# A third token tile whose low and high parts share one stationary operand

## The chip, the cores and the metric

The kernel runs on one core of a Trainium2 chip. The metric is the device time of one execution in microseconds (us), the median over runs. TensorE (PE) does the matmuls, with its weight loads (PEld) beside them; VectorE (DVE) and ScalarE (ACT) do the elementwise work; GpSimd (POOL) and SyncE (SP) mostly issue DMAs.

## What is computed

One inference step of a two-layer trunk for 256 prompt tokens and 8 x 8 sample tokens, 320 in all, model width 1024, in fp32. Each layer has a mixing sub-layer and a channel sub-layer, each followed by a LayerNorm of the scaled residual:

```python
mix, nb_a, nb_b, h_last = token_mixing(x, ...)      # convolution, recurrent and cross-attention branches,
                                                    # merged by gates, then merged @ w_mix_out
x = layer_norm(ALPHA * x + mix, ln1_g[l], ln1_b[l])
if l % 2 == 0:
    f = swiglu(x, w_ff_gate[j], w_ff_up[j], w_ff_down[j])   # hidden width 2816
else:
    f = moe_swiglu(x, w_router[j], ...)                     # top 2 of 8 experts
x = layer_norm(ALPHA * x + f, ln2_g[l], ln2_b[l])
```

## The kernel before

**Precision by parts.** An fp32 operand is cut into a high part (a cast to fp32r, made by ScalarE) and a low part (the operand less its high part, made by VectorE). A product is three matmuls that add up in PSUM: high x high, high x low, low x high. The product low x low is left out. The weights come in units of 128 rows x 1024 columns (512 KB) through a ring of 6 slots, which SyncE fills (L643). `make_hi` (L543) and `make_lo` (L551) split a unit into `wh` and `wl`, of which there are 3 (`SPLITS`): the high part of a unit may be made when the matmuls with the unit three before it are done.

**Two kinds of products.** Most products (`blocks`, L1660 to L1662) give their result with features on the partitions and the 320 tokens in the free dimension. Three of them have tokens on the partitions, so that the residual and the LayerNorm can work along a row; `rows_of` (L1665) does these: merged @ w_mix_out of each layer (8 units, called "mix") and hidden @ w_ff_down of layer 0 (22 units, "down"). In these the activations are the stationary operand and the weights the moving one.

**Token tiles.** `TOK = [0, 128, 192]` are the first tokens of three tiles of 128. Tile 2 holds tokens 192 to 319. Its first 64 rows (`DUP`) are tokens that tile 1 has too, and what is computed for them is used by nobody; the 64 sample tokens are its rows 64 to 127. For each unit, tile and half of 512 columns, `unit` issues three matmuls of 128x512 (L1673 high x high, L1674 high x low, L1675 low x high): 18 for a unit. Each tile and half has a PSUM bank, 6 in all. The tiles are taken in the order `TURN = (2, 0, 1)`. For all units but the last three (`LAST = 3`) the loop over tiles is the inner one; then each tile in turn takes its last three units and is closed, so that VectorE can begin with tile 2 while TensorE is at tiles 0 and 1.

**What follows a tile's close.** `residual` on VectorE (L1155) does, for each tile in the same order, x = ALPHA * x + bank for the two halves (L1161), the statistics (L1112, L1114), a wait for ScalarE's square root (`layer_norm_std`, L622; its square root L628, and a first tiny activation at L625 that brings the function table in early), the reciprocal (L1119), and the normalisation (L1120). TensorE then transposes x (`turn_x`, L1702), all 8 blocks of a tile behind each other, in the order of `TURN`; the later tiles overwrite the columns of the duplicated tokens. VectorE goes on with the splits of the next units (L555) and with `turned_lo`, which makes gain and bias (`xaff`, L1149) and the low part `xTl` (L1142) of the transposed rows.

**The stationary operands.** `mgh` and `mgl` (merged, [128, 8, 320]) and `hTh` and `hTl` (hidden, [128, 22, 320]) are separate tensors. ScalarE makes the high parts, one copy of 128x320 each (L976 for merged, L993 and L996 for hidden), VectorE the low parts in one subtraction each (`merged_lo` L1403, `hidden_lo` L1169). merged is made while TensorE is at the last branch product ("yb", 8 blocks of 24 matmuls), hidden during the feed-forward stretch of layer 0 (gate and up, 44 units of 24 matmuls). All these buffers lie in one arena by offsets written out by hand; tensors whose lives do not overlap share a place.

The order of the work is written out: `make_plan` counts the steps of TensorE, and `split_for(step)` on ScalarE and VectorE puts the splits of the coming units at fixed places in those engines' order.

Of the kernel before, what the change touches and what calls it, by code (L numbers as in the profile page):

```python
# [36 lines left out]
P = 128  # L37
# [35 lines left out]
MEAN_AFTER = 2  # L73
LAST = 3
# [194 lines left out]
def trunk(nc, x0, x0T, chan, rows, hist, stream, router_w, router_b, experts,  # L269
# [5 lines left out]
    with ExitStack() as ctx:  # L275
# [83 lines left out]
        v, mgh = share(JB * T, ("mgh", KT, T))  # L359
        ua, ig, ig_flat = blocks_of(v, JA, LEN_A), blocks_of(v, JB, T), v  # L360
# [16 lines left out]
        v, meml, mgl = share(JB * T, ("meml", KT, N_MEM), ("mgl", KT, T))  # L377
# [17 lines left out]
        hTh, hTl = cut_r("hTh", FT * T, FT), cut_r("hTl", FT * T, FT)  # L395
        dsig = cut(2 * T, 2)
        dlin = cut(2 * T, 2)
        dh = cut(2 * T, 2)
        xaff = cut(3 * T, 3)

# [63 lines left out]
        hgh_ready, hgl_ready = sem("hgh_ready"), sem("hgl_ready")  # L464
        mgh_ready, mgl_ready = sem("mgh_ready"), sem("mgl_ready")
# [156 lines left out]
        def layer_norm_std(act, n):  # L622

            act.wait_ge(eps_ready, 1)
            act.activation(turn_top[0:1], ones[0:1, 0:1], ACT.Sqrt)  # L625
# [197 lines left out]
        def _(act):  # L823
# [30 lines left out]

            for l in range(DEPTH):
# [117 lines left out]
                for n in range(KT):  # L973
                    split_for(tile_of(l, "yb", n).done)
                    act.wait_ge(mg_ready, KT * l + n + 1)
                    act.copy(mgh[:, n], mg[:, n]).then_inc(mgh_ready, 1)  # L976
                split_for(last_rows(l, "mix", KT))
                layer_norm_std(act, 2 * l)
                if l % 2 == 0:
# [4 lines left out]
                    for f in range(FT):  # L984
# [5 lines left out]
                        if f:  # L990
                            split_for(tile_of(l, "u", f - 1).done)
                            emptied(act, l, "u", f - 1)
                            act.copy(hTh[:, f - 1], dh[:, (f - 1) % 2]).then_inc(dhh_ready, 1)  # L993
                    split_for(tile_of(l, "u", FT - 1).done)
                    emptied(act, l, "u", FT - 1)
                    act.copy(hTh[:, FT - 1], dh[:, (FT - 1) % 2]).then_inc(dhh_ready, 1)  # L996
                    split_for(last_rows(l, "down", FT))
                    layer_norm_std(act, 2 * l + 1)
# [94 lines left out]
        def _(dve):  # L1093
# [61 lines left out]
            def residual(n, l, name):  # L1155

                for t in TURN:
                    for c in range(2):
                        m = 2 * t + c
                        filled(dve, l, name, m)  # L1160
                        frees(dve.scalar_tensor_tensor(out=x[:, t, 512 * c:512 * c + 512],  # L1161
                                                       in0=x[:, t, 512 * c:512 * c + 512], scalar=ALPHA,
                                                       in1=bank(l, name, m), op0=ALU.mult, op1=ALU.add), l, name, m)
                    for c in range(2):
                        emptied(dve, l, name, 2 * t + c)
                    spread(n, x, t)
                    scaled(n, x, t)

            def hidden_lo(f):  # L1169

                dve.wait_ge(dhh_ready, f + 1)
                dve.tensor_tensor(hTl[:, f], dh[:, f % 2], hTh[:, f].bitcast(F32), ALU.subtract)\
                   .then_inc(dhl_ready, 1)
# [933 lines left out]
```

## Time and profile before

| | us |
|---|---|
| median of 3 runs | 2064.41 (2064.2 to 2066.55) |
| the profiled execution | 2060.36 |
| its span, first to last instruction | 2058.6 |
| TensorE busy | 1923.8 (93%) |
| VectorE busy | 1488.0 (72%) |
| ScalarE busy | 1057.3 (51%) |
| mean granted TensorE clock | 0.973 of full speed |

How to read the rows further down: a line such as L1673 is one of the kernel. In a row of the busy time by stretch stand the stretch, its length, then for PE, PEld, DVE, ACT and POOL the busy us and the number of instructions in brackets, then the granted TensorE clock, the DMA engines' busy share and GB/s. A row of the timeline gives the start, the duration, and in square brackets the idle time before it with what ended it. Matmuls are pipelined: the duration of one is longer than the distance to the start of the next. A row of a group gives after the bar the busy time in us and the mean ns of one instruction. In the chain a row gives start, us on the chain, and what.

### The profile page before, as it was taken

Reading aid. Unit: us, or ns where it says so; the run is one execution under the profiler, and the core shown is the slowest. Engines: PE = TensorE matmul, PEld = TensorE weight load, DVE = VectorE, ACT = ScalarE, POOL = GpSimd, SP = SyncE. Lnnn points to the kernel's source line nnn. Section 1 sums busy time; section 2 is a strip of 40 time slices with the busy share of each in tenths; the row PEclk is TensorE's granted clock in tenths of the full one; section 3 lists DMA queues with packets and bytes.
Section 4 is the critical chain, followed back from the end, with each engine's and each line's share of the span. In section 5 each row is a group of like instructions: output and inputs, shape, how many; then the busy total and the mean of one; then the engine's idle time right before and its main releaser. Section 6 shows DMA issues by size and latency. Waiting matters only on the chain.

```text
span 2058.6 us, 27972 instructions
## 1 busy us (share of the span) xinstructions
PE 1923.8 (93%) x10429; PEld 1636.0 (79%) x10430; DVE 1488.0 (72%) x2049; ACT 1057.3 (51%) x1154; POOL 95.9 (5%) x156
## 2 busy tenths in 40 slices
PE   7999889899997999988979999999999999999990
PEld 7889789799986978988966677878788888876670
DVE  6987685665525888657567567888888888886664
ACT  4453643334322435364335446677777677765541
POOL 1100000000001000000000001010101010100000
PEclk9999999999999999999989999999999999999995
DMA  7643334354432553533437558898989898986413
GB/s 259 221 171 132 131 121 151 105 170 153 145 131 95 186 198 122 185 112 126 135 146 264 198 211 321 338 379 338 375 330 384 334 377 337 377 338 241 179 59 120
DMA packets 118741, 447.43 MB, mean 217 GB/s; under 512 B 10384, under 2 KB 10384, under 8 KB 118144
## 3 DMA queue, kind: packets, MB, share of 16 engines
q1 hardware_dynamic: 112416, 424.97, 56.5%
q0 software_dynamic: 6240, 21.33, 2.9%
q8 instruction: 53, 0.87, 0.2%
q14 instruction: 32, 0.26, 0.0%
HBM read 437.52 MB, written 11.36 MB: 218 GB/s over the span
## 4 chain that ended last, share of the span: by engine, by line
PE 76%; DVE 13%; issue 5%; ACT 5%; DMA 1%; SPq 0%; DVEq 0%; POOL 0%; ACTq 0%; POOLq 0%
PE psum L1896 11%; PE psum L1898 11%; PE psum L1897 10%; PE psum L1660 8%; PE psum L1661 8%; PE psum L1662 8%; PE psum L1646 4%; PE psum L1902 3%; PE psum L1903 3%; DVE wl L555 2%; DVE arena L1103 2%; PE psum L1673 2%; PE psum L1675 2%; PE psum L1674 2%; ACT wph L597 1%
## 5 line engine op out<-in xcount | busy, mean ns | idle before, releaser
L603 DVE TENSOR_TENSOR wpl<-e_ring,wph 128x2048 fp32r<-128x2048 f32 x269 | 605.5, 2285 | 84.9 <-ACT wph L597 84.0
L597 ACT CAST wph<-e_ring 128x2048 fp32r<-128x2048 f32 x269 | 502.1, 1905 | 118.8 <-PE psum L1898 66.8
L555 DVE TENSOR_TENSOR wl<-ring,wh 128x1024 fp32r<-128x1024 f32 x234 | 285.6, 1223 | 256.5 <-ACT wh L549 255.1
L1660 PE MATMUL psum<-xTh,wh 128*128 128x320 f32 x1184 | 379.6, 321 | 41.4 <-DVE wl L555 18.5
L1661 PE MATMUL psum<-xTl,wh 128*128 128x320 f32 x1184 | 372.2, 314 | 0.0
L1662 PE MATMUL psum<-xTh,wl 128*128 128x320 f32 x1184 | 372.1, 314 | 0.0
L549 ACT CAST wh<-ring 128x1024 fp32r<-128x1024 f32 x234 | 244.0, 1045 | 165.4 <-PE psum L1675 85.5
L1896 PE MATMUL psum<-wph,xe 128*128 128x512 f32 (+1 forms) x768 | 293.1, 382 | 2.0 <-issue 1.7
L1898 PE MATMUL psum<-wpl,xe 128*128 128x512 f32 (+1 forms) x768 | 288.5, 376 | 0.0
L1897 PE MATMUL psum<-wph,xe 128*128 128x512 f32 (+1 forms) x768 | 288.5, 376 | 0.0
L1660 PEld LDWEIGHTS psum<-xTh,wh 128*128 128x128 f32 x1184 | 228.2, 193 | 46.0 <-DVE wl L555 25.7
L1661 PEld LDWEIGHTS psum<-xTl,wh 128*128 128x128 f32 x1184 | 228.7, 193 | 0.6
L1662 PEld LDWEIGHTS psum<-xTh,wl 128*128 128x128 f32 x1184 | 228.0, 193 | 0.0
L1103 DVE SCALAR_TENSOR_TENSOR arena<-arena,par 128x256 f32<-128x256 f32 x576 | 179.7, 381 | 1.0
L1896 PEld LDWEIGHTS psum<-wph,xe 128*128 128x128 f32 x768 | 144.1, 188 | 32.2 <-issue 2.2
L1898 PEld LDWEIGHTS psum<-wpl,xe 128*128 128x128 f32 x768 | 144.0, 188 | 29.2
L1897 PEld LDWEIGHTS psum<-wph,xe 128*128 128x128 f32 x768 | 144.2, 188 | 27.8
L1896 PE MATMUL psum<-wph,hT 128*128 128x512 f32 x352 | 140.9, 400 | 5.3 <-DVE hT L1589 5.3
L1898 PE MATMUL psum<-wpl,hT 128*128 128x512 f32 x352 | 139.2, 395 | 0.0
L1897 PE MATMUL psum<-wph,hT 128*128 128x512 f32 x352 | 139.1, 395 | 0.0
L1896 PEld LDWEIGHTS psum<-wph,hT 128*128 128x128 f32 x352 | 66.0, 187 | 28.6 <-DVE wpl L603 4.5
L917 ACT ACTIVATE arena<-psum,par 128x320 f32<-128x320 f32 x48 | 25.3, 528 | 106.2 <-PE psum L1662 106.1
(305 smaller groups left out, 2600.6 us busy)
## 6 DMA issues: line engine op xcount, KB each, us to landing
e_ring<-experts SPq DMA_DIRECT2D x264, 1024.0 KB, 6.0
ring<-stream SPq DMA_DIRECT2D x274, 512.0 KB, 3.3
lnp<-rows POOLq DMA_DIRECT2D x4, 1024.0 KB, 5.7
arena<-out_rows SPq DMA_DIRECT2D x6, 512.0 KB, 8.0
x<-x POOLq DMA_DIRECT2D x3, 512.0 KB, 6.4
arena<-x0T SPq DMA_DIRECT2D x2, 640.0 KB, 5.9
o_a<-arena POOLq DMA_DIRECT2D x2, 540.0 KB, 8.6
o_k<-arena POOLq DMA_DIRECT2D x2, 512.0 KB, 6.3
```

The costliest lines, as they stand in the source:

```text
L549: act.copy(wh[:, q % SPLITS, :], ring[:, u % SLOTS, :]).then_inc(hi_done, 1)
L555: dve.tensor_tensor(wl[:, q % SPLITS, :], ring[:, u % SLOTS, :], wh[:, q % SPLITS, :].bitcast(F32), ALU.subtract).then_inc(lo_done, 1)
L597: act.copy(wph[:, SLOT_OF[m % NPOS], :], ring_place(m).rearrange("p u c -> p (u c)")).then_inc(hi_e, 1)
L603: dve.tensor_tensor(wpl[:, s, :], ring_place(m).rearrange("p u c -> p (u c)"), wph[:, s, :].bitcast(F32), ALU.subtract).then_inc(lo_e, 1)
L1103: return dve.scalar_tensor_tensor(out=out, in0=in0, scalar=scalar, in1=in1, op0=ALU.mult, op1=ALU.add)
L1646: return pe.matmul(out, lhs, rhs, start=(k == 0), stop=(k == n - 1), **kw)
L1660: pe.matmul(out, h[:, k], hi[:, k], start=(k == 0), stop=False)
L1661: pe.matmul(out, h[:, k], lo[:, k], start=False, stop=False)
L1662: ins = pe.matmul(out, low[:, k], hi[:, k], start=False, stop=(k == kt - 1))
L1896: pe.matmul(out, hi, h, start=first, stop=False, skip_group_check=True)
L1897: pe.matmul(out, lo, h, start=False, stop=False, skip_group_check=True)
L1898: return pe.matmul(out, hi, low, start=False, stop=final, skip_group_check=True)
```

## The change

- In `rows_of`, tile 2 takes as its stationary operand 128 columns of which the first 64 are the low part of the 64 sample tokens and the last 64 their high part. It is multiplied with the high and with the low part of the weights, two matmuls for a half in place of three. The duplicated tokens are no longer computed, and the product low x low of the sample tokens comes in. Tiles 0 and 1 are as before.
- PSUM rows 0 to 63 of tile 2's banks then hold the low half's sum, rows 64 to 127 the high half's. ScalarE copies rows 0 to 63 of each bank to rows 64 to 127 of `lo_rows` in SBUF (in `layer_norm_std`, after tile 2's close and before the function table is brought in) and signals `lo_moved`. VectorE waits for that before its residual of tile 2, does it on rows 64 to 127, and adds `lo_rows` (64x1024) before the statistics.
- High and low part lie in one tensor, `merged` [128, 8, 640] and `hidden` [128, 22, 640]: low part of the prompt (256 columns), low of the samples (64), high of the samples (64), high of the prompt (256). So ScalarE makes a high part with two copies (256 and 64 columns) and VectorE a low part with two subtractions.
- In the arena, ua/ig move next to the place of mgl, so that `merged` covers both; xaff moves; lo_rows takes the place of gg.

```diff
@@ -71,6 +71,7 @@
 MEAN_AFTER = 2
+TAIL, HEAD = T, T + NSAMP
@@ -356,8 +357,6 @@
             return v[:, 0:a * n].rearrange("p (a b) -> p a b", a=a)
-        v, mgh = share(JB * T, ("mgh", KT, T))
-        ua, ig, ig_flat = blocks_of(v, JA, LEN_A), blocks_of(v, JB, T), v
@@ -374,7 +373,10 @@
         pp, mg = blocks_of(v, 10, N_MEM), blocks_of(v, KT, T)
-        v, meml, mgl = share(JB * T, ("meml", KT, N_MEM), ("mgl", KT, T))
+        merged = place("merged", [P, KT, 2 * T], arena_at + 4 * off[0], F32R)
+        v = cut(JB * T)
+        ua, ig, ig_flat = blocks_of(v, JA, LEN_A), blocks_of(v, JB, T), v
+        v, meml = share(JB * T, ("meml", KT, N_MEM))
@@ -392,11 +394,14 @@
         off[0] = 0
-        hTh, hTl = cut_r("hTh", FT * T, FT), cut_r("hTl", FT * T, FT)
+        hidden = place("hidden", [P, FT, 2 * T], arena_at, F32R)
+        cut(2 * FT * T)
...
         dh = cut(2 * T, 2)
+        off[0] = ARENA - 4 * JB * T - T
         xaff = cut(3 * T, 3)
+        lo_rows = gg_flat[:, 0:D]
@@ -462,6 +467,7 @@
         hgh_ready, hgl_ready = sem("hgh_ready"), sem("hgl_ready")
+        lo_moved = sem("lo_moved")
@@ -619,9 +625,14 @@
             return nv
-        def layer_norm_std(act, n):
+        def layer_norm_std(act, n, l=None, name=None):
             act.wait_ge(eps_ready, 1)
+            if name:
+                for c in range(2):
+                    filled(act, l, name, 4 + c)
+                    act.copy(lo_rows[DUP:P, 512 * c:512 * c + 512], bank(l, name, 4 + c)[0:DUP])\
+                       .then_inc(lo_moved, 1)
@@ -851,6 +862,11 @@
                 filled(act, *key)
+
+            def hidden_hi(f):
+
+                act.copy(hidden[:, f, HEAD:2 * T], dh[:, f % 2, 0:SEQ]).then_inc(dhh_ready, 1)
+                act.copy(hidden[:, f, TAIL:HEAD], dh[:, f % 2, SEQ:T]).then_inc(dhh_ready, 1)
@@ -973,9 +989,10 @@
                     act.wait_ge(mg_ready, KT * l + n + 1)
-                    act.copy(mgh[:, n], mg[:, n]).then_inc(mgh_ready, 1)
+                    act.copy(merged[:, n, HEAD:2 * T], mg[:, n, 0:SEQ]).then_inc(mgh_ready, 1)
+                    act.copy(merged[:, n, TAIL:HEAD], mg[:, n, SEQ:T]).then_inc(mgh_ready, 1)
                 split_for(last_rows(l, "mix", KT))
-                layer_norm_std(act, 2 * l)
+                layer_norm_std(act, 2 * l, l, "mix")
@@ -990,12 +1007,12 @@
                             emptied(act, l, "u", f - 1)
-                            act.copy(hTh[:, f - 1], dh[:, (f - 1) % 2]).then_inc(dhh_ready, 1)
+                            hidden_hi(f - 1)
...
                     emptied(act, l, "u", FT - 1)
-                    act.copy(hTh[:, FT - 1], dh[:, (FT - 1) % 2]).then_inc(dhh_ready, 1)
+                    hidden_hi(FT - 1)
                     split_for(last_rows(l, "down", FT))
-                    layer_norm_std(act, 2 * l + 1)
+                    layer_norm_std(act, 2 * l + 1, l, "down")
@@ -1158,19 +1175,27 @@
                         filled(dve, l, name, m)
-                        frees(dve.scalar_tensor_tensor(out=x[:, t, 512 * c:512 * c + 512],
-                                                       in0=x[:, t, 512 * c:512 * c + 512], scalar=ALPHA,
-                                                       in1=bank(l, name, m), op0=ALU.mult, op1=ALU.add), l, name, m)
+                        if t == 2:
+                            dve.wait_ge(lo_moved, 2 * n + c + 1)
+                        at = slice(DUP if t == 2 else 0, P)
+                        frees(dve.scalar_tensor_tensor(out=x[at, t, 512 * c:512 * c + 512],
+                                                       in0=x[at, t, 512 * c:512 * c + 512], scalar=ALPHA,
+                                                       in1=bank(l, name, m)[at], op0=ALU.mult, op1=ALU.add),
+                              l, name, m)
...
                         emptied(dve, l, name, 2 * t + c)
+                    if t == 2:
+                        link(dve.tensor_tensor(x[DUP:P, t, :], x[DUP:P, t, :], lo_rows[DUP:P], ALU.add))
...
             def hidden_lo(f):
-                dve.wait_ge(dhh_ready, f + 1)
-                dve.tensor_tensor(hTl[:, f], dh[:, f % 2], hTh[:, f].bitcast(F32), ALU.subtract)\
-                   .then_inc(dhl_ready, 1)
+                dve.wait_ge(dhh_ready, 2 * f + 2)
+                dve.tensor_tensor(hidden[:, f, 0:SEQ], dh[:, f % 2, 0:SEQ], hidden[:, f, HEAD:2 * T].bitcast(F32),
+                                  ALU.subtract)
+                dve.tensor_tensor(hidden[:, f, SEQ:T], dh[:, f % 2, SEQ:T], hidden[:, f, TAIL:HEAD].bitcast(F32),
+                                  ALU.subtract).then_inc(dhl_ready, 1)
@@ -1402,10 +1427,12 @@
                 def merged_lo(n):
-                    dve.wait_ge(mgh_ready, KT * l + n + 1)
+                    dve.wait_ge(mgh_ready, 2 * (KT * l + n + 1))
                     dve.wait_ge(mg_ready, KT * l + n + 1)
-                    dve.tensor_tensor(mgl[:, n], mg[:, n], mgh[:, n].bitcast(F32), ALU.subtract)\
-                       .then_inc(mgl_ready, 1)
+                    dve.tensor_tensor(merged[:, n, 0:SEQ], mg[:, n, 0:SEQ], merged[:, n, HEAD:2 * T].bitcast(F32),
+                                      ALU.subtract)
+                    dve.tensor_tensor(merged[:, n, SEQ:T], mg[:, n, SEQ:T], merged[:, n, TAIL:HEAD].bitcast(F32),
+                                      ALU.subtract).then_inc(mgl_ready, 1)
@@ -1662,7 +1689,7 @@
                 step(ins)
-            def rows_of(l, name, nk, hi, lo, made):
+            def rows_of(l, name, nk, both, made):
@@ -1670,9 +1697,15 @@
                         out, cs = bank(l, name, 2 * t + c), slice(512 * c, 512 * c + 512)
-                        pe.matmul(out, hi[:, k, r0:r0 + P], h[:, cs], start=(k == 0), stop=False)
-                        pe.matmul(out, hi[:, k, r0:r0 + P], low[:, cs], start=False, stop=False)
-                        ins = pe.matmul(out, lo[:, k, r0:r0 + P], h[:, cs], start=False, stop=(k == nk - 1))
+                        if t == 2:
+                            lo_hi = both[:, k, SEQ:HEAD]
+                            pe.matmul(out, lo_hi, h[:, cs], start=(k == 0), stop=False)
+                            ins = pe.matmul(out, lo_hi, low[:, cs], start=False, stop=(k == nk - 1))
+                            continue
+                        lo, hi = both[:, k, r0:r0 + P], both[:, k, HEAD + r0:HEAD + r0 + P]
+                        pe.matmul(out, hi, h[:, cs], start=(k == 0), stop=False)
+                        pe.matmul(out, hi, low[:, cs], start=False, stop=False)
+                        ins = pe.matmul(out, lo, h[:, cs], start=False, stop=(k == nk - 1))
@@ -1820,14 +1853,14 @@
                                            start=True, stop=True))
-                rows_of(l, "mix", KT, mgh, mgl, lambda k: pe.wait_ge(mgl_ready, KT * l + k + 1))
+                rows_of(l, "mix", KT, merged, lambda k: pe.wait_ge(mgl_ready, KT * l + k + 1))
...
                                 blocks((l, w, n), xTh, xTl, T, turned=KT if (w, n) == ("g", 0) else None)
-                    rows_of(l, "down", FT, hTh, hTl, lambda f: pe.wait_ge(dhl_ready, f + 1))
+                    rows_of(l, "down", FT, hidden, lambda f: pe.wait_ge(dhl_ready, f + 1))
```

## Rows read from the trace of the kernel before

**Rows 1.** The page's chain that ended last, by engine
```profile
PE 76%; DVE 13%; issue 5%; ACT 5%; DMA 1%; SPq 0%; DVEq 0%; POOL 0%; ACTq 0%; POOLq 0%
```

**Rows 2.** Busy by stretch (PE, PEld, DVE, ACT, POOL, PEclk, DMA, GB/s): mix, down, mix
```profile
357.00:391.00 34.00, 34.00 (x151) 27.60 (x150) 17.47 (x25) 9.25 (x12) 0.00 (x0) 1.00 0.35 117
...
558.00:650.00 92.00, 92.00 (x396) 74.02 (x395) 32.81 (x37) 23.45 (x25) 0.00 (x0) 1.00 0.36 120
...
1012.00:1045.00 33.00, 33.00 (x145) 26.75 (x144) 16.87 (x24) 8.84 (x12) 0.00 (x0) 1.00 0.34 116
```

**Rows 3.** Chain around the end of layer 0's mix (start, us, what)
```profile
382.82 1.30 DVE x L1161 x2
...
387.11 1.21 DVE x L1161 x2
...
391.32 1.20 DVE x L1161 x2
...
395.51 2.29 DVE wl L555 x2
```

**Rows 4.** Timeline: first and last matmul of layer 0's mix, and of down
```profile
357.53 0.40 PE L1673 MATMUL psum<-wh,mgh 128*128 128x512 f32 x1
...
390.62 0.39 PE L1675 MATMUL psum<-wh,mgl 128*128 128x512 f32 x1
...
557.92 0.39 PE L1673 MATMUL psum<-wh,hTh 128*128 128x512 f32 x1
...
650.08 0.39 PE L1675 MATMUL psum<-wh,hTl 128*128 128x512 f32 x1
```

**Rows 5.** Timeline, 378 to 380 us: the last unit's split
```profile
378.35 0.40 PE L1673 MATMUL psum<-wh,mgh 128*128 128x512 f32 x1
...
378.60 1.05 ACT L549 CAST wh<-ring 128x1024 fp32r<-128x1024 f32 x1 [3.11 <-PE psum L1675]
...
379.67 1.28 ACT L625 ACT_TABLE_LOAD   x1
...
379.69 1.23 DVE L555 TENSOR_TENSOR wl<-ring,wh 128x1024 fp32r<-128x1024 f32 x1 [2.94 <-ACT wh L549]
```

**Rows 6.** Groups by shape: ScalarE and VectorE (xcount, busy us, mean ns)
```profile
L1037 ACT COPY arena<-psum 32x512 f32<-32x512 f32 x10 | 5.8, 577 | 53.0 <-PE psum L1903 45.5 <-DMA out_rows<-arena,rows_out 7.5
...
L911 ACT COPY arena<-psum 128x512 f32<-128x512 f32 x10 | 5.1, 607 | 0.0
...
L1131 DVE TENSOR_TENSOR x<-x,lnp 128x1024 f32<-128x1024 f32 x12 | 14.5, 1219 | 2.2 <-PE psum L1702 2.2
...
L825 ACT ACTIVATE arena<-psum,par 128x256 f32<-128x256 f32 x16 | 7.6, 474 | 50.5 <-PE psum L1662 50.5
...
L825 ACT ACTIVATE arena<-psum,par 128x64 f32<-128x64 f32 x24 | 7.5, 311 | 15.2 <-PE psum L1662 15.2
...
L917 ACT ACTIVATE arena<-psum,par 128x320 f32<-128x320 f32 x48 | 25.3, 528 | 106.2 <-PE psum L1662 106.1
...
L1227 DVE TENSOR_SCALAR arena<-arena,par 128x256 f32<-128x256 f32 x16 | 6.5, 407 | 0.0
...
L1227 DVE TENSOR_SCALAR arena<-arena,par 128x64 f32<-128x64 f32 x16 | 4.9, 307 | 0.0
...
L1329 DVE TENSOR_SCALAR arena<-arena,par 128x320 f32<-128x320 f32 x8 | 3.0, 441 | 0.1
```

**Rows 7.** Busy time by stretch: feed-forward of layer 0, and yb
```profile
404.00:558.00 154.00, 153.77 (x1043) 153.35 (x1043) 91.74 (x116) 62.54 (x90) 0.54 (x1) 1.00 0.45 154
...
320.00:357.00 37.00, 37.00 (x256) 37.00 (x255) 20.98 (x30) 14.44 (x21) 0.00 (x0) 1.00 0.44 146
```

**Rows 8.** Busy time by stretch: after layer 0's mix
```profile
399.00:405.00 6.00, 5.52 (x19) 4.71 (x19) 5.87 (x14) 3.13 (x8) 0.00 (x0) 0.50 0.33 106
```

**Rows 9.** Timeline: tile 1's transposes after each layer's mix
```profile
395.57 1.10 PE L1702 MATMUL psum<-ident,x 128*128 128x128 f32 x8 [1.58 <-DVE x L1120]
...
1050.21 1.81 PE L1702 MATMUL psum<-ident,x 128*128 128x128 f32 x8 [1.59 <-DVE x L1120]
```

## The prediction, made before the changed kernel had run

> **What bounds the kernel now.** I read the page's chain first, then the busy time by stretch, then the chain of waits around each row-wise product, and last the durations by shape. TensorE carries 76% of the chain that ended last, VectorE 13% [rows 1]. Those shares are averages over the whole kernel, so the stage decides. In the stretches that hold the three row-wise products (mix of layer 0, down of layer 0, mix of layer 1) TensorE is busy without a gap, while VectorE and ScalarE have half of the time or more to spare [rows 2]. So a matmul taken out there shortens the stretch, up to the point at which another engine takes over.
>
> Another does, at the end of each product. The third token tile (tile 2) is closed first, then tiles 0 and 1. VectorE starts its residual for tile 2 right behind that tile's last matmul, at 382.82, and never pauses after it: tile 0 at 387.11, tile 1 at 391.32, the next weight splits at 395.51 [rows 3]. A tile costs VectorE 4.2 to 4.3 us and costs TensorE 18 matmuls, 4.2 us. The two run level, and from tile 2's close on the chain is VectorE's. The reader should see this: matmuls removed before that close bring it forward at full price; work added on VectorE, or in front of it, after that close is paid in full.
>
> **Part 1, the matmuls removed.** Per unit of 128 rows of weights, tile 2 took 2 halves x 3 matmuls and will take 2 x 2. The units are 8 + 22 + 8 = 38, so 76 matmuls of 128x512 go, and as many weight loads, all ahead of tile 2's close. The duration shown for one, 0.40 us, is not its price, since they overlap; the distance between starts is. In mix of layer 0 the first of 144 starts at 357.53 and the last at 390.62: 33.09 / 143 = 0.231 us. In down, 396 from 557.92 to 650.08: 92.16 / 395 = 0.233 us [rows 4]. Mix of layer 1 has the same form and no gap either [rows 2]; I take 0.231. Gain: 32 x 0.231 + 44 x 0.233 = **17.7 us**.
>
> The Trainium skill, "TensorE: Matmul & The Clock Gate", section "Back-to-back issue gap", puts a sustained stream of weight loads and matmuls at about 131 ns for each matmul of 512 columns, and an isolated gap at about 216 ns. The trace does not agree with the first and is near the second; by 131 ns the estimate for the removed matmuls would be 76 x 0.131 = 10.0 us.
>
> **Part 2, a stall at the last unit.** The split of the last unit is let go by the end of unit n-4, the last before the closing section. In layer 0's mix the closing section starts at 378.35; ScalarE makes the high part at 378.60 (1.05 us), VectorE the low part at 379.69 (1.23 us), so it is there at 380.92 [rows 5]. Tile 2 now has 12 matmuls for the two units ahead of the last, and comes to it at 378.35 + 2.77 = 381.1, just after. With 8 it comes at 380.2 and waits about 0.75 us. Down and layer 1's mix have the same order of work; three products: **+2.25 us**. Bounds: 0 to 1 us each. In all other units a split has two whole units of 16 x 0.231 = 3.7 us for its 2.3 us, so nothing waits.
>
> **Part 3, tile 2's tail.** ScalarE now copies the low half's sum (64x512) of each bank to SBUF, VectorE's residual waits for it, and an add over 64x1024 follows. Fewer lanes do not shorten a row: a 32x512 copy takes 577 ns, a 128x512 one 607 [rows 6]. First copy: +0.6 us before VectorE can start. The second runs under the first residual, of which two take 1.30 us [rows 3]: +0. The add has the form of the tensor-tensor on x, 1219 ns [rows 6], and the statistics wait for it: +1.22, and some 0.08 for its semaphore. That is 1.9 us, x3 = **+5.7 us**, exposed because nothing stands still in rows 3. Bounds: 1.2 (the add alone) to 2.6 us (both copies in front) each. ScalarE's table load (1.28 us [rows 5]) moves behind the copies; it ends some 2.8 us after tile 2's close, and the square root that needs it is asked for 2.9 us after it now and 4.8 us then: hidden; if not, a few tenths.
>
> **Part 4, copies and subtractions cut in two.** 38 high parts on ScalarE and 38 low parts on VectorE become 256 + 64 columns. On ScalarE the nearest rows give 474 + 311 against 528 ns, on VectorE 407 + 307 against 441 [rows 6]: about +0.26 us each, 10 us on each engine in all. They lie under TensorE, which is busy 153.77 of 154 us in the feed-forward stretch, with VectorE at 92 and ScalarE at 63, and 37 of 37 in the yb stretch [rows 7]. If that cover were gone they would cost up to 10 us. I take 0. The buffers that change place (xaff, ua/ig, merged, hidden) issue no further instruction and no DMA, and nothing is moved past the queues of SyncE and GpSimd. The new wait on VectorE (lo_moved) has the tile's whole tail behind it, priced above; ScalarE's new wait on tile 2's close has only the table load behind it.
>
> **Part 5, the clock.** The tail grows by 1.9 us in which TensorE has only transposes. Now, after its last dense matmul at 390.62 and 24 transposes with gaps, the granted clock is 0.50 (1.2 GHz) from 399 to 405 [rows 8]. Tile 1's 8 transposes took 1.10 us at the full clock after layer 0's mix, and 1.81 us after layer 1's, where the clock was already down [rows 9]. Coming 1.9 us later, they may fall under the low clock in the other two products too: 0 to 0.7 us each, I take 0.3: **+0.6 us**.
>
> **Sum:** -17.7 + 2.25 + 5.7 + 0.6 = **-9.1 us**, against the profiled execution's 2060.36 us (span 2058.6): 2051.3. The three runs shown have a median of 2064.41, 4.1 us above the profiled one; I take the change over as it stands: **2055.3 us**.
>
> **The rivals.**
> (a) The tail is hidden after all. Then only the matmuls count: 2064.4 - 17.7 = 2046.7. For it: VectorE idles before tile 2's residual. Against it: after that it never pauses [rows 3]. Chance 0.08, with partial forms near 2050.
> (b) The change gives little. A removed matmul may give back less than the distance between starts, if something other than its columns sets that; the nearest smaller distance is that of the 320-column ones, about 0.147 us (1043 in 153.8 us [rows 7]). 76 x 0.147 = 11.2, less 8.55 for parts 2, 3 and 5, is 2.6 us: 2061.8. Against it: both long stretches agree within 0.002 us. Or parts 2, 3 and 5 all come at their upper bounds: -17.7 + 3 + 7.8 + 1.4 = -5.5. Chance of ending within 0.2%: 0.10.
> The skill's 131 ns would land here too, at an estimate of 1.4 us gained.
> (c) Slower. The longer tail makes each of the three restarts of TensorE stay at the low clock for longer, where its matmuls take up to twice as long, so half of the added stretch is lost. To be 4 us slower it must cost 13 us beyond my sum, 26 us more at 0.50, nearly 9 at each restart, where now it is about 6 [rows 8]. It would decide from there; at 10 us each the time is 2055.3 + 15 = 2070. For it: each tail ends in such a stretch already. Against it: 1.9 us is little beside that. Chance 0.01.
> (d) The change doesn't do what it says, with TensorE waiting at every unit for a split. It would have to be bound by 2.3 us of split work in a unit of 3.7 us. Were it so, the units would stay at 4.2 us and only the costs remain: 2073. Chance 0.01.
>
> **How the numbers follow.** Forecast 0.80, (a) 0.08, (b) 0.10, (c) and (d) 0.02. About 0.2% (4.1 us) is what a measurement of this kernel can tell from no change, so faster 0.88, within it 0.10, slower 0.02. The range: at the low end part 3 at 1.2 us and no stall, -17.7 + 3.6 = -14.1, 2050.3; at the high end -5.5 as under (b), 2058.9, and a microsecond more because the runs shown spread over 2.4 us. I give 2050 to 2060.
>
> **What would show it.** The stretch of down from first to last matmul at 92.2 - 10.3 + 0.7 = 82.6 us, each mix at 33.1 - 3.7 + 0.7 = 30.1; a wait of 0.7 us of TensorE on the low part of the last unit, three times; from tile 2's close to tile 1's normalised rows 12.7 + 1.9 = 14.6 us; no new wait in the feed-forward stretch. It is wrong if VectorE idles between tiles 2 and 0, if the distance between matmuls changes, or if the clock stays at 0.50 well past where it did.

## The result, and the profile after

The changed kernel is slower: 2086.19 us, median of 7 runs (2077.47 to 2090.51), against 2064.41 for the kernel before, 7 runs (2059.43 to 2066.55). The ratio is 1.0103, with a 95% interval of 1.0086 to 1.012. The forecast was 2055.3, and 0.02 stood on slower. (Where an experiment below is compared with the kernel before, that kernel was timed again beside it: 2061.6 to 2062.9.)

The page of the changed kernel: span, busy time, the instruction queue, and the chain that ended last by engine (answers to [rows 1] and to the table of before).

```profile
span 2085.8 us, 27914 instructions
...
PE 1931.1 (93%) x10353; PEld 1639.2 (79%) x10354; DVE 1493.6 (72%) x2090; ACT 1063.8 (51%) x1198; POOL 100.6 (5%) x156
...
q14 instruction: 67, 0.55, 0.1%
...
PE 72%; DVE 13%; issue 8%; ACT 5%; DMA 2%; DVEq 0%; SPq 0%; POOL 0%; ACTq 0%; POOLq 0%
```

The same queue on the page of the kernel before:

```profile
q14 instruction: 32, 0.26, 0.0%
```

Two things are out of place. TensorE has 76 matmuls fewer and is busy 7 us longer: its mean granted clock is 0.960, where it was 0.973. And "issue" (time in which the engine waited for nothing that the profile shows) has gone from 5% of the chain to 8%, while the packets of code on queue 14 have doubled, from 32 to 67.

**Where the prediction looked, it came out.** The changed kernel's timeline at the end of layer 0's mix (answers to [rows 3, 5]):

```profile
378.06 1.05 ACT L555 CAST wh<-ring 128x1024 fp32r<-128x1024 f32 x1 [2.67 <-PE psum L1708]
...
379.14 1.22 DVE L561 TENSOR_TENSOR wl<-ring,wh 128x1024 fp32r<-128x1024 f32 x1 [2.49 <-ACT wh L555]
...
379.43 0.40 PE L1703 MATMUL psum<-wl,merged 128*128 128x512 f32 x1
380.51 0.47 PE L1702 MATMUL psum<-wh,merged 128*128 128x512 f32 x1 [0.68 <-DVE wl L561]
...
381.76 1.06 ACT L634 COPY arena<-psum 64x512 f32<-64x512 f32 x2 [2.66 <-PE psum L1703]
...
382.47 1.30 DVE L1181 SCALAR_TENSOR_TENSOR x<-x,psum 64x512 f32<-64x512 f32 x2 [2.11 <-ACT arena L634]
...
382.84 1.28 ACT L636 ACT_TABLE_LOAD   x1
...
383.88 1.22 DVE L1188 TENSOR_TENSOR x<-x,arena 64x1024 f32<-64x1024 f32 x1
...
385.13 1.29 DVE L1129 BATCH_NORM_STATS2 stats<-x 128x6 f32<-128x512 f32 x2
```

And its chain around the same place, from the third tile's close:

```profile
381.76 0.59 ACT arena L634
...
388.07 1.29 DVE x L1181 x2
...
392.36 1.20 DVE x L1181 x2
...
396.56 2.28 DVE wl L561 x2
```

The reader should see each predicted step: TensorE's wait on the last low part (0.68 us); the copy (0.59) in front of the residual; the second copy under it; the add (1.22). From tile 2's close at 381.7 to the next split at 396.56 it is 14.8 us, where 14.6 was forecast.

**Where the time came from.** The whole span cut at places that every kernel here has: first and last matmul start of each row-wise product, and the end of each turn (one pass of the loop over experts in layer 1, whose mark is VectorE's tiny memset `turn_end`). The last column is experiment e12, below.

| stretch, us | before | changed | e12 |
|---|---|---|---|
| start to mix of layer 0 | 357.5 | 359.2 | 359.4 |
| mix of layer 0 | 33.09 | 30.42 | 30.42 |
| to down | 167.3 | 169.4 | 169.4 |
| down | 92.16 | 82.81 | 82.81 |
| to mix of layer 1 | 362.1 | 367.5 | 363.4 |
| mix of layer 1 | 33.11 | 30.43 | 30.42 |
| to the end of turn 1 | 202.9 | 204.0 | 204.8 |
| turn 2 | 100.7 | 103.4 | 100.6 |
| turns 3 to 7 | 499.6 | 528.7 | 499.7 |
| turn 8 and the end | 210.1 | 209.9 | 209.8 |
| sum: the span | 2058.6 | 2085.8 | 2050.8 |

Up to the end of turn 1 the changed kernel is 4.3 us ahead. It then loses 2.6 us in turn 2 and 29.1 us in turns 3 to 7, which compute nothing that the change touches. (The stretch to layer 1's mix is 360 to 365 us in kernels that leave that part as it was, and the stretch from the start to the first mix is 357.5 to 362.8 us over all profiles, so a single profile says little about either.)

VectorE's waits from 1060 us to the end (waiting line, what for, us in total, times, longest). Changed:

```profile
DVE arena L1582 <- ACT arena L1055: 53.8, 12, 9.4
DVE arena L1585 <- issue: 42.7, 5, 9.5
DVE arena L1585 <- ACT arena L1055: 24.0, 23, 7.9
```

Before (L1558 is the same instruction as L1585):

```profile
DVE arena L1555 <- ACT arena L1038: 53.5, 12, 9.0
DVE arena L1558 <- ACT arena L1038: 34.4, 18, 4.8
```

At a turn's start VectorE's first instruction used to wait for ScalarE; in the changed kernel it stands idle 8.5 us (42.7 / 5) although that input is there. The timeline of the changed kernel at the start of turn 3 shows how this reaches TensorE:

```profile
1347.20 0.06 DVE L1652 MEMSET turn_end<- 128x1 f32 x1
...
1350.59 0.60 ACT L1055 ACTIVATE arena<-psum 128x512 f32<-128x512 f32 x1 [2.95 <-PE psum L1931]
...
1355.76 0.40 PE L1931 MATMUL psum<-wpl,xe 128*128 128x512 f32 x1
1357.49 0.73 PE L1967 MATMUL psum<-zero 128*128 128x512 f32 x2 [1.34 <-DVE arena L1585]
1360.47 1.86 PE L1673 MATMUL psum<-values,lnp 128*128 128x2 f32 x12 [2.24 <-DVE lnp L1544]
...
1362.85 0.63 PE L1930 MATMUL psum<-wph,xe 128*128 128x512 f32 x1
```

The kernel before at the same place:

```profile
1348.86 0.06 DVE L1625 MEMSET turn_end<- 128x1 f32 x1
...
1352.24 0.60 ACT L1038 ACTIVATE arena<-psum 128x512 f32<-128x512 f32 x1 [2.95 <-PE psum L1898]
...
1352.87 0.69 DVE L1558 TENSOR_TENSOR arena<-psum,arena 128x512 f32<-128x512 f32 x1 [3.95 <-ACT arena L1038]
```

Before, VectorE goes on 0.63 us after ScalarE's result has begun. Changed, it goes on at 1356.75 (its row has 9.49 us of idle time put down to issue), 6.2 us after. TensorE runs out of matmuls at 1356.2, idles twice, and its clock falls. The changed kernel's busy time by stretch there:

```profile
1347.00:1357.00 10.00, 9.15 (x40) 7.01 (x38) 0.51 (x3) 5.63 (x6) 1.91 (x2) 1.00 0.90 327
1360.00:1366.00 6.00, 5.53 (x21) 4.73 (x22) 6.00 (x6) 1.69 (x1) 0.00 (x0) 0.50 0.80 274
```

In the kernel before the stretch 1345 to 1366 is busy for all 21 us at a clock of 1.00. The DMA view of 1330 to 1360 shows the code packets. Changed:

```profile
DMA packets 2644, 9.92 MB, mean 331 GB/s; under 512 B 227, under 2 KB 227, under 8 KB 2639
...
q14 instruction: 5, 0.04, 0.5%
```

Before, queue 14 does not appear in that stretch: code is fetched five packets at a time where the changed kernel starts a turn. 67 - 32 = 35 more in all is 5 on average for each of the seven returns to the loop's head.

The times of the packets tie the two together. In turn 3 of the changed kernel code packets start on queue 14 at 1347.5, 1353.1 and 1354.7, and VectorE goes on at 1356.75, 2.0 us after the last of them. It is so at each of the 22 turn starts at which VectorE's idle time is put down to issue (5 here, 5 in e4, 6 each in e1 and e10 below): VectorE goes on 1.9 to 2.0 us after a code packet has started.

### The profile page after: what moved, and what is told of

The parts are those of the page before. It is cut to its first block, busy times and chain, and to the rows that moved or that the text cites. A ratio compares the mean times of both kernels' runs of the same rounds, so it can differ in the third digit from the quotient of the medians.

```text
span 2085.8 us, 27914 instructions
## 1 busy us (share of the span) xinstructions
PE 1931.1 (93%) x10353; PEld 1639.2 (79%) x10354; DVE 1493.6 (72%) x2090; ACT 1063.8 (51%) x1198; POOL 100.6 (5%) x156
## 4 chain that ended last, share of the span: by engine, by line
PE 72%; DVE 13%; issue 8%; ACT 5%; DMA 2%; DVEq 0%; SPq 0%; POOL 0%; ACTq 0%; POOLq 0%
PE psum L1929 10%; PE psum L1930 9%; PE psum L1931 9%; PE psum L1687 9%; PE psum L1688 8%; PE psum L1689 8%; PE psum L1673 4%; PE psum L1935 3%; PE psum L1936 3%; DVE wl L561 2%; DVE arena L1120 2%; DVE wpl L609 1%; PE psum L1708 1%; PE psum L1706 1%; PE psum L1707 1%
## 5 line engine op out<-in xcount | busy, mean ns | idle before, releaser
L1929 PE MATMUL psum<-wph,xe 128*128 128x512 f32 (+1 forms) x768 | 298.6, 389 | 3.1 <-issue 2.8
L1930 PE MATMUL psum<-wph,xe 128*128 128x512 f32 (+1 forms) x768 | 293.3, 382 | 0.0
L1931 PE MATMUL psum<-wpl,xe 128*128 128x512 f32 (+1 forms) x768 | 292.9, 381 | 0.0
L1929 PEld LDWEIGHTS psum<-wph,xe 128*128 128x128 f32 x768 | 147.4, 192 | 34.3 <-issue 3.3
L1930 PEld LDWEIGHTS psum<-wph,xe 128*128 128x128 f32 x768 | 147.4, 192 | 28.7
```

The source lines that it names most:

```text
L1929: pe.matmul(out, hi, h, start=first, stop=False, skip_group_check=True)
L1930: pe.matmul(out, lo, h, start=False, stop=False, skip_group_check=True)
L1931: return pe.matmul(out, hi, low, start=False, stop=final, skip_group_check=True)
```

## The experiments

**The question.** Nothing in the loop over experts was edited. What the change did to it is to move it: counted in the compiled program, waits and branches included, the loop begins at instruction 1660 of VectorE's program before and at 1707 after (+47: 38 second subtractions, 6 waits, 3 adds), at 958 and 1005 of ScalarE's (+47), and at 6013 and 5937 of TensorE's (-76). It is 292 instructions long on VectorE and 270 on ScalarE. The theory: the loop's place in an engine's program decides whether its code is read again in each turn with the engine waiting. Rivals: the change does it by its buffers, by the tail, or by the clock. The means is an "empty" instruction, one that only counts up a semaphore for which nothing waits, spread over the 22 passes of the feed-forward loop of layer 0, where both engines have time:

```diff
+        pad = sem("pad")
                         emptied(dve, l, "u", f)
                         if f:
                             hidden_lo(f - 1)
+                        for _ in range(48 // FT + (f < 48 % FT)):
+                            dve.sem_inc(pad, 1)
```

Each count below is of places moved. "+47" on VectorE puts the loop of the kernel before where the changed kernel has it.

**e1: kernel before, VectorE +47.**

> The kernel before, with 48 instructions that only count up a semaphore put into VectorE's program in the feed-forward stretch, so that the loop over the experts stands 47 places later in VectorE's program, as in the changed kernel. The changed kernel reads five packets of 8192 bytes of code in each turn of that loop, the kernel before none. Theory A (the place of the loop in VectorE's code decides whether it is read anew each turn): code packets in every turn, VectorE idle for up to 9 us at a turn's start, the clock at 0.5 behind it, about 2086 to 2091. Theory B (the same with ScalarE's program): no change, 2064. Theory C (the longer tail behind each row-wise product, through the clock): no change, 2064.

Measured: 2091.17 us, 1.015 (1.0125 to 1.0175) of the kernel before: with none of the change in it, the whole loss and more. VectorE's waits from 1060 us on, and the page's instruction queue:

```profile
DVE arena L1561 <- issue: 49.3, 6, 8.7
```

```profile
q14 instruction: 67, 0.55, 0.1%
```

**e2: kernel before, ScalarE +47** (the same edit with `act`).

> The kernel before, with 47 such instructions in ScalarE's program, which moves its loop over the experts by 47 places, as in the changed kernel. Theory A: no change, 2064. Theory B: code packets in every turn and 2086 to 2091. Theory C: no change, 2064. If both programs matter, this and the run with VectorE's program share the code packets of the changed kernel between them.

Measured: 2061.76, ratio 0.9996 (0.9984 to 1.0007), 32 packets. ScalarE's place does not matter here.

**e3: changed kernel, VectorE moved on to 1788, +128 against before.**

> The changed kernel, with 82 such instructions in VectorE's program in the feed-forward stretch, so that its loop stands 128 places (8192 bytes, the size of one code packet) later than in the kernel before, not 47. Theory A: the code packets of VectorE in the turns go, and with them 25 to 35 us: 2052 to 2060, near the forecast of 2055. Theory B: no change against the changed kernel, 2086. Theory C: the same, 2086.

Measured: 2056.78, ratio 0.9982 (0.9972 to 0.9991), 33 packets. VectorE's waits from 1060 us on no longer have an issue line, and the first instruction waits for ScalarE as in the kernel before:

```profile
DVE arena L1588 <- ACT arena L1056: 36.8, 18, 7.2
```

The experts' first weight load comes at 1071.3 instead of 1079.9, 8.6 us earlier, near the 9.1 forecast; a single profile shows this with the spread of its first stretch in it (e11 has 1076.2).

**e4: changed kernel, ScalarE +81.**

> The changed kernel, with 81 such instructions in ScalarE's program, so that ScalarE's loop stands 128 places later than in the kernel before. Theory A: no change, 2086. Theory B: 2052 to 2060. Theory C: no change, 2086.

Measured: 2082.79, ratio 1.0107 (1.0084 to 1.0131), 68 packets: it stays slow, and VectorE is idle on issue for 8.3 us at five turn starts. Together e1 to e4 leave VectorE's place alone as the cause of turns 3 to 7.

**e5: the changed kernel at 1788 without the low sum.** The two copies, the waits for them and the add are left out, so low part x weights is missing from the three products' result for the 64 sample tokens.

```diff
-                for c in range(2):
-                    filled(act, l, name, 4 + c)
-                    act.copy(lo_rows[DUP:P, 512 * c:512 * c + 512], bank(l, name, 4 + c)[0:DUP])\
-                       .then_inc(lo_moved, 1)
...
-                        if t == 2:
-                            dve.wait_ge(lo_moved, 2 * n + c + 1)
...
-                    if t == 2:
-                        link(dve.tensor_tensor(x[DUP:P, t, :], x[DUP:P, t, :], lo_rows[DUP:P], ALU.add))
```

> The changed kernel with its loop 128 places on from the kernel before (91 instructions put in) and without what follows tile 2's close: no copy of the low half's sum, no wait for it, no add. So the product of the low part of the 64 sample tokens is left out of the result. If the copy and the add are paid in full three times, as the prediction has it, this is 5.7 us below the run with the same place of the loop and the sum (2056.8): about 2051, and tile 2's close to the end of tile 1's normalisation takes 12.7 us, not 14.6. If they are hidden, it is 2056.8.

Measured: 2049.69, ratio 0.9934 (0.9913 to 0.9954), 7.1 us under e3 (predicted for Part 3: 5.7). In its trace the stretch from mix of layer 0 to down is 167.5 us; with the low sum it is 169.4. That is 1.9 us for one tail, the predicted size. The stretches with the other two tails are shorter than in e3 by 1.3 us (down to mix of layer 1) and 2.6 us (mix of layer 1 to the end of turn 1): 5.8 us for the three.

**e6: the change in down alone, VectorE at 1788.** mgh and mgl and the mix products stay as before; in `rows_of`, `residual` and `layer_norm_std` the new form is taken for "down" only.

> The change in the down product alone (22 units, 44 matmuls), both mix products as in the kernel before; 104 instructions put in, so that VectorE's loop stands 128 places on. By the prediction's terms: -10.3 for the matmuls, +0.75 for the stall at the last unit, +1.9 for the tail, +0.3 for the clock: -7.3 against the kernel before (2061.8), 2054.5. The two mix products then gave 16 x 0.231 - 2.95 = 0.75 us each in the full change, so this should be no slower than the aligned full change by more than 1.5 us. If the lower clock behind each longer tail costs more than I put down, the down product alone comes out below the full change's 2056.8.

Measured: 2053.35, ratio 0.9954 (0.9939 to 0.9969). Down holds 44 of the 76 removed matmuls and one of the three tails, so it gives most of the gain for a third of the cost. It comes out below e3, which the expectation would have put down to a dearer clock. e12 below shows a nearer reason: e3 takes 103.2 us for turn 2, and this kernel 100.4.

**e7 and e8: kernel before, VectorE +23 and +95, one run each.**

> The kernel before with VectorE's loop moved by 23 places. The loop is 292 instructions long, 2.3 packets of 128. If it is read anew when it touches four packets and not when it touches three, only 35 of 128 places are bad, and 47 is one of them: then at most one or two of the moves by 23, 63 and 95 are bad. If any move off the old place is bad, all three are: 2088. Read by the code packets: 32 in all where the loop stays, 67 where it is read in each turn.

> The kernel before with VectorE's loop moved by 95 places. If four packets touched are what decides, 47 being bad and 0 (or 128) good, this is most likely good: 2062 and 32 or 33 code packets. If any place off the old one is bad: 2088 and 67.

Measured: 2061.86 and 2059.79, 32 packets both. The kernel before took 2058.7 to 2065.3 beside them. So more instructions alone cost nothing that a run can show; it is the place.

**e9: the change in down alone, nothing added** (loop at 1685, +25).

> The change in down alone, with nothing added to VectorE's program for its place: the experts' loop then starts 25 instructions later than in the kernel before (instruction 1685, where the kernel before has 1660, the changed one 1707). Place theory: 23 later cost nothing, so 25 later should cost nothing either; VectorE does not idle before a turn's first residual, some 33 code packets on queue 14, and the time is that of the same change with the loop at 1788, about 2053 to 2056 us. Rival, size theory (every instruction added before the loop costs a little, and 128 later is an accident): 25 of 47 instructions give about half of the 29 us, 2068 to 2072 us, and over 40 packets.

Measured: 2053.10, ratio 0.9958 (0.9945 to 0.9972), 32 packets. The size theory (2068 to 2072) is out.

**e10: kernel before, VectorE +63, one run.**

> The kernel before with 64 empty instructions on VectorE in the feed-forward loop, so that the experts' loop starts 63 later, at 1723. 23 and 95 later cost nothing, 47 later costs 29 us. If the bad places are those where the 292 instructions of the loop touch four packets of 128 instead of three (35 places of 128), this one can be bad or good, and it tells on which side of 47 the bad stretch lies. Bad: 67 packets on queue 14, VectorE idle 8 to 9 us before each of 5 or 6 turns, about 2090 us. Good: 32 or 33 packets and about 2062 us. Any value between, say 2075 us, would speak against a loop that either fits or doesn't.

Measured: 2114.58, 67 packets. Bad, and by more than was expected of either place: I had taken all bad places to cost the same. Its waits on VectorE:

```profile
DVE arena L1561 <- issue: 65.8, 6, 12.9
```

The same number of packets, 11.0 us a time (65.8 / 6) instead of 8.2. The packets' times show the difference: at the start of turn 3 the last two before VectorE goes on start 5.0 us apart (1363.6 and 1368.6, VectorE at 1370.6), in e1 only 1.8 us apart (1356.1 and 1357.9, VectorE at 1359.9). Why they are further apart at this place is not shown.

**e11: changed kernel, VectorE at 1755, +95.**

> The changed kernel whole, with 49 empty instructions on VectorE, so that the experts' loop starts at 1755, 95 later than in the kernel before; there, 95 later was as fast as nothing. Place theory: the idle time before the turns goes, 33 packets on queue 14, and the time is that of the changed kernel with the loop at 1788, 2054 to 2059 us. Rival (the changed kernel wants 128 later for another reason, its own instructions in the loop): it stays near 2085 us.

Measured: 2056.66, ratio 0.9969 (0.9957 to 0.9982), 32 packets. The changed kernel is cured at a second place, as the theory wants.

It left one thing open. Turn 2 took 103.4 us here, as in every profile with both mix products changed (103.2 to 103.4), against 100.1 to 100.7 in the others in which VectorE does not idle there. TensorE's timeline at the start of turn 2 in e11:

```profile
1243.88 0.49 PE L1932 MATMUL psum<-wph,xe 128*128 128x512 f32 x1 [2.87 <-issue]
```

and in the kernel before:

```profile
1246.43 0.49 PE L1896 MATMUL psum<-wph,xe 128*128 128x512 f32 x1 [1.74 <-issue]
```

Soon after it, in e11, eight matmuls in a row start 0.43 us apart instead of 0.23. TensorE's program had also been moved, by the 76 matmuls taken out.

**e12: e11 with 76 empty instructions at the head of TensorE's program**; its loop is back at 6013.

```diff
+            for _ in range(76):
+                pe.sem_inc(pad_pe, 1)
             pe.wait_ge(const_ready, 6)
             for l in range(DEPTH):
```

> The changed kernel whole, VectorE's loop at 1755 as in e11, and now TensorE's too: 76 empty instructions at the head of TensorE's program, where it waits 7.4 us for the first rows, put its experts' loop back to instruction 6013, where the kernel before has it (5937 without them). In every profile with both mix products changed TensorE waits 2.6 to 2.9 us on its own issue when the second turn starts, in every other one 1.2 to 1.7 us, and the second turn takes 103.2 to 103.4 us against 100.3 to 100.8. Place theory for TensorE: the wait falls to 1.2 to 1.7 us, the second turn to about 100.5 us, and the time to some 2.9 us under e11, 2053 to 2054 us. Rival (the change itself, by its buffers or the clock, costs the second turn those 2.9 us): the turn stays at 103.3 us and the time near 2056.7 us, or a little above it, if the 76 instructions cost something at the start.

Measured: 2052.93, ratio 0.9958 (0.9943 to 0.9973), 3.7 us under e11. The intervals of the two ratios overlap, so it is the trace that shows the 2.8 us of turn 2. That turn now takes 100.6 us, and the row is

```profile
1238.79 0.50 PE L1935 MATMUL psum<-wph,xe 128*128 128x512 f32 x1 [1.63 <-issue]
```

The 76 instructions were not hidden at the start: TensorE's first matmul comes at 12.6 us, in the other profiles at 7.1 to 7.6. The stretch to mix of layer 0 is 359.4 us all the same, within the spread of the others. The other instruction queue, 8, carries 53 packets in every profile, so no count of packets shows TensorE's wait. That its code is behind it is argued: from e12, and from e6 and e9, where 44 matmuls fewer stand ahead of the loop and the wait is 1.4 us, turn 2 100.4.

All of it side by side, by the place of VectorE's loop:

| kernel | place | us | code packets | VectorE idle at a turn's start, "issue" |
|---|---|---|---|---|
| before | 1660 | 2061.8 | 32 | none |
| e2, before, ScalarE +47 | 1660 | 2061.8 | 32 | none |
| e7, before +23 | 1683 | 2061.9 | 32 | none |
| e9, down alone | 1685 | 2053.1 | 32 | none |
| changed | 1707 | 2086.2 | 67 | 8.5 us x5 |
| e4, changed, ScalarE +81 | 1707 | 2082.8 | 68 | 8.3 us x5 |
| e1, before +47 | 1707 | 2091.2 | 67 | 8.2 us x6 |
| e10, before +63 | 1723 | 2114.6 | 67 | 11.0 us x6 |
| e8, before +95 | 1755 | 2059.8 | 32 | none |
| e11, changed | 1755 | 2056.7 | 32 | none |
| e12, changed, TensorE +76 | 1755 | 2052.9 | 32 | none |
| e3, changed | 1788 | 2056.8 | 33 | none |
| e5, changed without the low sum | 1788 | 2049.7 | 33 | none |
| e6, down alone | 1788 | 2053.4 | 33 | none |

Shown: the place of VectorE's loop by itself makes the loss (e1) and takes it away (e3, e11). e3 and e11 have the buffers and the tails of the changed kernel, so those two rivals are out, and the clock with them. Putting TensorE's loop back took away the 2.8 us of turn 2 (e12). Shown as well: extra code packets come with the loss each time, and VectorE goes on 1.9 to 2.0 us after one of them. That it is the branch back to the loop's head which finds its code gone is the reading of these rows, not shown step by step. The Trainium skill, "Runtime: NRT & Kernel Launch", section "Instruction fetch mechanics", says that a taken branch whose target is not in what the engine holds forces a fetch before it can go on, and the trace agrees as far as it shows, with 5 packets and 8.2 to 11.0 us a turn. The same section of the Trainium skill describes the store of such an engine as one of 512 instructions, filled in order in blocks of 256. By an estimate from these figures a loop of 292 reaches into a third block from 35 of 256 starting places, and the bad and good places above can be so divided. They can be divided as well by packets of 128 instructions (8.2 KB, as queue 14 carries them), with 35 bad places in 128, as in the expectation of e7. What stays open is the rule for a bad place; the bad stretch holds 1707 and 1723 and lies between 1685 and 1755.

## Why the prediction was wrong

**The step that failed** is in Part 4: the added copies and subtractions "lie under TensorE, which is busy 153.77 of 154 us ... I take 0", and with it the sum, which had a term for the time of each added instruction and none for its place in the program. The time was covered, as said: e5, which has the added copies and subtractions but no tail, takes 167.5 us from mix of layer 0 to down, the kernel before 167.3, and from the first matmul of yb to the first of mix it is 27.95 us in both. But 47 instructions on VectorE moved the loop behind them, and that cost about 29 us over turns 3 to 7; 76 matmuls fewer moved TensorE's and cost 2.6 to 2.8 us in turn 2. "Nothing is moved past the queues" was true of DMAs and overlooked the code. Neither rival (c) nor any other case had this mechanism. It could have been asked of the profile of before: the page has a queue of code (32 packets), and layer 1 is a loop run eight times.

**Part 1, the matmuls: right.** The three products went from 33.09 + 92.16 + 33.11 us to 30.42 + 82.81 + 30.43, down 14.7 us; adding back the 2.8 us of stall that the same stretches show (Part 2), the matmuls gave 17.5 where 17.7 was forecast. The distance between matmuls stayed at 0.23 us, so the first form of rival (b) is out, and with it the estimate of 10.0 us by the 131 ns of the Trainium skill.

**Part 2, the stall: right in kind, a little small.** In each of the three products the last unit's first matmul starts 1.08 us after the one before it instead of 0.23, and the next one 0.31 us after that: 0.92 us, 2.8 in all against 2.25. The wait shown is 0.68 us; the rest is that TensorE starts again more slowly.

**Parts 3 and 5, the tail and the clock.** From the last matmul of layer 0's mix to the first of down: 167.3 us before, 169.4 after, so 2.1 us; 1.9 for the tail and 0.3 for the clock had been taken. e5 isolates 1.9. The longer tail does pull the clock down. Busy time by stretch, before and changed:

```profile
393.00:400.00 7.00, 2.60 (x20) 2.15 (x18) 6.56 (x12) 3.21 (x6) 0.00 (x0) 0.89 0.29 81
...
393.00:400.00 7.00, 4.91 (x20) 3.92 (x20) 6.46 (x11) 2.72 (x5) 0.00 (x0) 0.53 0.15 48
```

Tile 2's fifth transpose before, and then in the changed kernel, with tile 1's eight (answer to [rows 8, 9]; tile 1's had taken 1.10):

```profile
391.97 0.33 PE L1702 MATMUL psum<-ident,x 128*128 128x128 f32 x1 [0.53 <-DVE x L1161]
...
393.01 0.33 PE L1735 MATMUL psum<-ident,x 128*128 128x128 f32 x1 [2.54 <-DVE x L1181]
...
396.61 1.97 PE L1735 MATMUL psum<-ident,x 128*128 128x128 f32 x8 [0.40 <-DVE x L1137]
```

TensorE now idles 2.54 us there where it idled 0.53, and the stretch 393 to 400 has a clock of 0.53 where it had 0.89. After layer 1's mix tail and clock together cost 1.8 us (34.6 us to the experts' first matmul before, 36.4 in e12).

**Rival (a)** (tail hidden) falls with e5. **Rival (c)** had the sign right and the cause wrong: the stretches behind the row-wise products grew by about 2 us each, tail and clock together, not by 9; the clock spells that cost time come after the turns' starts, and they follow VectorE's wait.

**The local sum stands.** With both loops put in good places the same change gives 2052.93 against 2061.83, -8.9 us (by the interval of its ratio, 11.8 to 5.6 us less), where the sum said -9.1. The traces say the same without the runs' times: from the first matmul of layer 0's mix to the end of turn 1 the six profiles with the products of the kernel before (before, e1, e2, e7, e8, e10) take 888.5 to 892.0 us (median 890.4), the five of the whole change (changed, e3, e4, e11, e12) 881.2 to 884.6 (median 881.6), 8.8 us less. The terms missed by little, and in part against each other: 0.2 us less for the matmuls, 0.5 more for the stall, and 5.9 for tails and clock together (14.7 less 8.8) where 6.3 was put down. The mechanism of the change was sized well; the price of where it put other code was missing.

## What to carry to other kernels

When an edit adds or removes instructions ahead of a loop that the engines really branch through, look at the changed kernel's instruction queue and at "issue" in the waits at the loop's head before judging the edit: here 47 more instructions on VectorE, whose own time was covered, and 76 fewer on TensorE turned a gain of 8.9 us into a loss of 21.8; about 29 us of that came by VectorE's place. If the packets have grown, move the loop with a few empty instructions in covered time and time it again. And price each piece of a change by itself: the form in down alone has 44 of the 76 matmuls and one tail of three, needs no such instruction, and at 2053.1 us is as fast as the whole change in its best place (2052.9).

## What was not expected of the hardware

- The place of a loop of 292 instructions in VectorE's program was worth 29 us (1.015, 1.0125 to 1.0175) at +47 and some 53 us at +63 (one run), and nothing that the runs show at +23, +95 and +128.
- The same shift on ScalarE, whose loop has 270 instructions, was worth nothing (0.9996, 0.9984 to 1.0007).
- A packet of code on queue 14 is 0.55 MB / 67 = 8.2 KB, and a VectorE that stood at a turn's start went on 1.9 to 2.0 us after one had started, 22 times of 22.
- VectorE standing 8 to 11 us becomes 3.7 to 10 us of a turn, since TensorE has matmuls for the first part of it and then pays again: after a pause its clock was 0.50 for some 6 us (0.43 us from matmul to matmul instead of 0.23).
